# Causal mask of the stick-breaking attention by a mask matmul in place of a diagonal-seeded scan

## The chip, the cores and the metric

The kernel runs on one core of one Trainium2 chip. The metric is the device time of one execution in microseconds (us), median of several runs. Engines: PE is TensorE, ACT is ScalarE, DVE is VectorE, POOL is GpSimd, SP issues DMAs.

## The reference

Two transformer-like blocks run on one sequence of 512 tokens with model width 1024: a hybrid block (forgetting attention, causal convolution, gated feed-forward), then a state-space layer, and last a stick-breaking attention layer with 16 heads of 64. Only that last layer is touched. For a query t and a key s, with z the scaled logit, it computes

```python
z = einsum('bthd,bshd->bhts', q[:, lo:hi], k[:, :hi]) * scale
mask = (lo + arange(128))[:, None] > arange(hi)[None, :]      # strictly earlier keys
log_keep = where(mask, log_sigmoid(-z), 0.0)
after = cumsum(log_keep, axis=3, reverse=True) - log_keep     # sum over later allowed keys
a = exp(where(mask, log_sigmoid(z) + after, -inf))
out = einsum('bhts,bshd->bthd', a, v[:, :hi])
```

So each weight is sigmoid(z) of its key times the product of sigmoid(-z) over the allowed keys that come after it. Queries go in blocks of 128, so a block has 128, 256, 384 or 512 keys, and only its last 128 columns (the diagonal block) hold masked places.

## The kernel before, in words

Everything is in one launch and one core. Matrix products are done in three passes on operands split into a high and a low part (fp32r). A panel of weights is 1 MB; panels stream from HBM into `raw`, ACT makes the high part (line 189), DVE the low part (line 193), PE multiplies.

The last part of the program (line 1974 on) first makes keys, values and the first queries (loop of nine panels, lines 2290 to 2308 on DVE), and then runs the attention as a pipeline, written out by hand, over 32 units. A unit n is a pair of heads t = n // 4 and a query block qb = n % 4; both heads (e = 0, 1) are done in it. The stages of a unit are:

- `logits` on PE (line 2076): six matmuls, three for each head, that contract 64 rows each; the two heads lie in the two row halves of the array. They write PSUM banks 2 and 3. The width is nk = 128 (qb + 1) keys, but at least 256. The last matmul increments `z_done`.
- ACT waits for `z_done`, writes sigmoid(z) into `sig` (line 2258, shown as tile x) and sigmoid(-z) into `rest` (line 2262), and increments `keep`. PE waits for `keep` of unit n before the logits of unit n + 1.
- DVE scans `rest` from the last key to the first (line 2346), one scan for each head. The scan computes state = rest * state + own, starting from 0. `own` is a [128, 512] tile with zeros in its first 384 columns and the identity in its last 128, so the state is 0 at the masked places, becomes 1 at the diagonal and is multiplied on from there. It increments `rest`.
- POOL multiplies `sig` by the scanned `rest` shifted by one key (line 2049) and increments `am`. Column 512 of `rest` is the value to the right of the last key: 0.
- PE transposes the product (`turn`, line 2086), ACT copies it to SBUF (`take`, line 2233), PE multiplies with the values (`values`, line 2100), and increments `pv_done`.

Around these stages PE has filling work: the remaining query and gate projections (`project`, line 2123, until unit 27) and, after them, the first products of the output projection (`out_early` and `out_part`, line 2132). In iteration n PE does: logits of n, two k-tiles of the filler (six matmuls of 512 columns), turn of n - 2, two more k-tiles, values of n - 3. What ends the filler halves on ACT and DVE is lines 2239 and 2244 (ACT) and 2321 and 2316 (DVE); the gate is line 2332 and the split of its result lines 2250 and 2337.

The tile `exact` holds the first four of five constant matrices rounded to fp32r: identity, an upper triangle, and two masks with -1e30. It is made once at the start (line 585). The mask `neg_after` is -1e30 where column > row; `neg_from` is -1e30 where column >= row, and is not used. The first attention of the program (units from 127 to 214 us) adds `neg_after` to its own logits in PSUM by a matmul with the identity as weights; its lines are 798, 802 and 805:

```python
for e in range(2):
    mm = pe.matmul(ps[:, 2 + e, qb * P:nk], ident_r, exact[:, CST["neg_after"], :],
                   start=False, stop=True, skip_group_check=True)
```

`own` shares the 2 KB of a partition that `exact` has (line 132), and is written over it by DVE before the second attention (lines 2287 to 2289).

Of the kernel before, what the change touches and what calls it, by code (L numbers as in the profile page):

```python
# [15 lines left out]
F32 = mybir.dt.float32  # L16
F32R = mybir.dt.float32r
ALU = mybir.AluOpType
# [3 lines left out]
P = 128  # L22
S = 512
# [7 lines left out]
HD = 64  # L31
# [46 lines left out]
CST = dict(ident=0, upper=1, neg_after=2, neg_from=3, ones=4)  # L78
# [21 lines left out]
def build(nc, x_in, panels, ada, vecs, cst, w_f, w_dt, x_kept, ac_rows, out):  # L100
    ctx = ExitStack()
    with ctx:
        def sem(name):
            return ctx.enter_context(nc.semaphore(name))

        def sbuf(scope, name, shape, dt=F32):
            return scope.enter_context(nc.sbuf_tensor(name, shape, dt))

        def shared_sbuf(scope, first, then):

            with nc.sbuf_tensor(*first) as tensor:
                pass
            return [tensor] + [sbuf(scope, *one) for one in then]
# [15 lines left out]
        eps = sbuf(ctx, "eps", [P, 1])  # L129
        quad = sbuf(ctx, "quad", [P, 1])  # L130

        exact, own = shared_sbuf(ctx, ("exact", [P, 4, P], F32R), [("own", [P, S], F32)])
        ps = ctx.enter_context(nc.psum_tensor("ps", [P, 8, S], F32))
        MODB = 4
        ident = consts[:, CST["ident"], :]
        ones = consts[:, CST["ones"], :]
        ident_r = exact[:, CST["ident"], :]

        def v(name, i=None, n=None):
            a, w = VEC[name]  # L140
            if i is None:
                return vec[:, a:a + w]
            return vec[:, a + i:a + i + (n or 1)]
# [47 lines left out]
        def split_lo(e, c, i):  # L191
            e.wait_ge(hi_split, at(c + 1, i))
            e.tensor_tensor(wlo[:, c % 2, :, :], raw[:, c % 2, :, :], whi[:, c % 2, :, :].bitcast(F32),  # L193
                            ALU.subtract).then_inc(lo_split, 1)
# [478 lines left out]
        with ExitStack() as kept:  # L673
            with ExitStack() as seg:
# [5 lines left out]
                u = sbuf(seg, "u", [P, CT, CK - 1 + S])  # L680
# [654 lines left out]
        with ExitStack() as seg:  # L1335
# [24 lines left out]
            k = 0  # L1360
# [613 lines left out]
        with ExitStack() as seg:  # L1974
# [4 lines left out]
            QS = 3  # L1979
# [8 lines left out]
            sig = x[:, 0:6, :].rearrange("p (a h) s -> p a h s", a=3)  # L1988
            og = x[:, 6:8, :]
            amt = ada_raw[:, 0, :, :].rearrange("p k n -> p (k n)").rearrange("p (a h s) -> p a h s", a=2, h=2)  # L1990
            z2 = ada_raw[:, 1, :, :].rearrange("p k n -> p (k n)").rearrange("p (a s) -> p a s", a=4)
            rest = sbuf(seg, "rest", [P, 2, 2, S + 1])
            h0 = rest[:, 0, :, 0:S]
            pre3 = pre_norm(v("kv_norm"), "kvsc", "kvsh", hhi, hlo, h0, ps[:, 7, :])
            pre4 = pre_norm(v("norm2", KT, KT), "ssc", "ssh", h2hi, h2lo, h0, ps[:, 7, :], slot=2)
            fin = counting(bank_done=KT - 1, x_new1=KT, sq_ready=KT, ss_used=KT, std_ready=1, rs_ready=1, spread=1,
                           out_ready=KT, out_stored=16 * KT)
            fsq = v2[:].rearrange("p a (b s) -> p (a b) s", b=2)
            B = {k: sem("b_" + k) for k in ("own", "z_done", "sig", "keep", "rest", "am", "t_done", "amt",
                                            "pv_done", "og", "ohi", "olo", "half", "khi", "qhi", "qfree", "zsig",  # L2000
                                            "zfree")}
            sb0 = FIRST["sb_out"]
# [2 lines left out]
            def place(j):  # L2005

                if j in (7, 8):
                    return c0 + 15 - j
                if j < 9 or j >= 16:
                    return c0 + j  # L2010
                return FIRST["z2"] + (j - 9) // 2 if j % 2 else FIRST["q2"] + (j - 8) // 2
# [6 lines left out]
            with nc.Block() as block:  # L2018
                @block.sync
                def _(sp):  # L2020
# [8 lines left out]
                    for j in range(6, 20):  # L2029
                        sp.wait_ge(lo_split, c0 + j - 1)  # L2030
                        sp.dma_start(raw[:, (c0 + j) % 2, :, :].rearrange("p t n -> p (t n)"),
                                     panels[place(j)]).then_inc(w_landed[(c0 + j) % 2], 16)
                    sp.wait_ge(B["t_done"], NU)
                    sp.wait_ge(B["olo"], KT)
                    sp.dma_start(x[:], x_kept).then_inc(x_back, 16)
# [6 lines left out]
                def _(pool):  # L2042
# [3 lines left out]
                    for n in range(NU):  # L2046
                        nk = (n % TB + 1) * P
                        pool.wait_ge(B["rest"], n + 1)
                        pool.tensor_tensor(sig[:, n % 3, :, 0:nk], sig[:, n % 3, :, 0:nk],  # L2049
                                           rest[:, n % 2, :, S - nk + 1:S + 1], ALU.mult).then_inc(B["am"], 1)  # L2050

                @block.tensor
                def _(pe):
# [9 lines left out]
                    def logits(n):  # L2063
                        t, qb = divmod(n, TB)
                        nk = (qb + 1) * P
                        nw = max(nk, 2 * P)
                        if n == 0:
                            pe.wait_ge(pair_free[1], (q0 + 7) // 2 + 2)
                        else:
                            pe.wait_ge(B["keep"], n)  # L2070
                        if qb == 0 and t >= 2:
                            pe.wait_ge(B["qfree"], t - 1)
                        for u, (q, k) in enumerate(((qhi, khi), (qhi, klo), (qlo, khi))):
                            for e in range(2):
                                r0 = HD * e
                                mm = pe.matmul(ps[:, 2 + e, 0:nw], q[r0:r0 + HD, t % QS, qb * P:nk],  # L2076
                                               k[r0:r0 + HD, t, 0:nw], start=u == 0, stop=u == 2, skip_group_check=True)
                        mm.then_inc(B["z_done"], 1)

                    def turn(n):  # L2080
# [93 lines left out]
                    for b in (5, 6, 7, 4):  # L2174
# [4 lines left out]
                        for k2i in range(2):  # L2179
                            mm = out_part(0, b, k2i)  # L2180
                    mm.then_inc(panels_used, 1)
                    for b in (5, 6, 7, 4):
                        for k2i in range(2):
                            mm = out_part(1, b, k2i)
# [3 lines left out]
                    for k2i in range(2):  # L2188
                        for b in range(8):
                            mm = out_part(2, b, k2i)  # L2190
# [3 lines left out]
                    for j, b in enumerate(ORDER):  # L2194
                        for k2i in range(2):
                            mm = out_part(3, b, k2i)
# [85 lines left out]
                def _(dve):  # L2282
# [1 line left out]
                    pre4["coefs"](dve)  # L2284
                    pre3["dve"](dve)
                    split_lo(dve, c0 + 1, 0)
                    dve.memset(own[:, 0:S - P], 0.0).then_inc(B["own"], 1)
                    dve.tensor_copy(own[:, S - P:S], ident).then_inc(B["own"], 1)
                    dve.memset(rest[:, :, :, S:S + 1], 0.0).then_inc(B["own"], 1)
                    for j in range(9):  # L2290
                        pair = (q0 + j) % 2
                        bank = ps[:, 2 * pair:2 * pair + 2, :]
# [13 lines left out]
                            pre4["dve"](dve, 4 * j, 4 * j + 4)  # L2306
                        if j == 7:
                            read_mod(dve, NADA - 2, NADA)
                    dve.wait_ge(B["own"], 3)

                    def turn_half(mh):
                        name, i, b, c = half_of(mh)
# [27 lines left out]
                    for n in range(NU + 6):  # L2340
                        if n < NU:
                            nk = (n % TB + 1) * P
                            dve.wait_ge(B["keep"], n + 1)
                            for e in range(2):
                                turned = rest[:, n % 2, e, S - nk:S][:, ::-1]
                                scan = dve.tensor_tensor_scan(turned, turned, own[:, S - nk:S][:, ::-1], 0.0,  # L2346
                                                              ALU.mult, ALU.add)
                            scan.then_inc(B["rest"], 1)
                        if n == 0:
                            split_lo(dve, c0 + 10, 0)  # L2350
                        if n >= STEPS and n % STEPS == 0 and n // STEPS <= HALVES:
                            turn_half(n // STEPS - 1)
                        if n >= 7 and (n - 3) % 4 == 0:
                            gate((n - 3) // 4 - 1)
                        if n >= 9 and (n - 5) % 4 == 0:
                            out_lo((n - 5) // 4 - 1)
# [119 lines left out]
```

## Time and profile before

| | |
|---|---|
| median of 3 runs | 1405.9 us (1403.95, 1405.9, 1407.66) |
| the profiled execution: its own time / its span | 1407.66 us / 1405.9 us |
| PE busy | 1340.1 us, 95% of the span |
| DVE, ACT, POOL busy | 821.7, 588.5, 409.5 us |
| the attention pipeline, 1198 to 1357 us | PE busy 157.36 of 159 us |

The profile is of one execution. Its span is what the instructions cover; its own time is the device time of the same execution, 1.8 us more. It is the slowest of the three runs. That its span has the same figure as the median is a coincidence. Busy times are summed over instructions that overlap in the pipeline of PE, so two matmuls in a row may each show 390 ns and start 230 ns apart; the start times tell what one costs.

### The profile page before, as it was taken

Reading aid. Unit: us, or ns where it says so; the run is one execution under the profiler, and the core shown is the slowest. Engines: PE = TensorE matmul, PEld = TensorE weight load, DVE = VectorE, ACT = ScalarE, POOL = GpSimd, SP = SyncE. Lnnn points to the kernel's source line nnn. Section 1 sums busy time; section 2 is a strip of 40 time slices with the busy share of each in tenths; the row PEclk is TensorE's granted clock in tenths of the full one; section 3 lists DMA queues with packets and bytes.
Section 4 is the critical chain, followed back from the end, with each engine's and each line's share of the span. In section 5 each row is a group of like instructions: output and inputs, shape, how many; then the busy total and the mean of one; then the engine's idle time right before and its main releaser. Section 6 shows DMA issues by size and latency. Waiting matters only on the chain. (4 is left out here: it accounts for less than half of the span.)

```text
span 1405.9 us, 19406 instructions
## 1 busy us (share of the span) xinstructions
PE 1340.1 (95%) x7840; PEld 1066.5 (76%) x7840; DVE 821.7 (58%) x966; ACT 588.5 (42%) x849; POOL 409.5 (29%) x191
## 2 busy tenths in 40 slices
PE   5999999889999999999999999999899999999996
PEld 3778867668888888887788876777787799777775
DVE  2789974576555554324657665787832842566643
ACT  4323656342222222122444447777632422555551
POOL 0000000149978879999100000000000050233310
PEclk9999999889999999999799999999999999999998
DMA  9434062115444455554132233334222342111121
GB/s 383 147 146 150 31 242 89 61 64 205 179 179 179 179 209 194 198 203 152 56 128 90 92 116 102 121 106 132 88 89 90 124 170 91 66 54 38 61 90 60
DMA packets 41350, 181.12 MB, mean 129 GB/s; under 512 B 3392, under 2 KB 20160, under 8 KB 21312
## 3 DMA queue, kind: packets, MB, share of 16 engines
q1 hardware_dynamic: 40128, 171.73, 34.0%
q10 hardware_dynamic: 1152, 8.39, 1.7%
q8 instruction: 51, 0.84, 0.2%
q14 instruction: 19, 0.16, 0.0%
HBM read 173.75 MB, written 6.36 MB: 128 GB/s over the span
## 5 line engine op out<-in xcount | busy, mean ns | idle before, releaser
L193 DVE TENSOR_TENSOR wlo<-raw,whi 128x2048 fp32r<-128x2048 f32 x95 | 253.1, 2665 | 171.0 <-ACT whi L189 168.5
L200 POOL TENSOR_TENSOR ada_raw<-ada_raw,cs 128x2048 f32<-128x2048 f32 x36 | 150.4, 4178 | 495.7 <-DVE h2lo L451 451.1
L271 PE MATMUL ps<-hhi,whi 128*128 128x512 f32 x640 | 252.0, 394 | 2.3 <-PEq L563 0.8
L271 PE MATMUL ps<-hhi,wlo 128*128 128x512 f32 x640 | 249.4, 390 | 0.0
L271 PE MATMUL ps<-hlo,whi 128*128 128x512 f32 x640 | 249.1, 389 | 0.0
L189 ACT ACTIVATE whi<-raw 128x2048 fp32r<-128x2048 f32 x95 | 181.6, 1912 | 144.4 <-PE ps L1312 91.3
L209 POOL TENSOR_TENSOR ada_raw<-ada_raw 128x1024 f32<-128x1024 f32 x72 | 164.4, 2283 | 5.6
L271 PEld LDWEIGHTS ps<-hhi,whi 128*128 128x128 f32 x640 | 120.2, 188 | 28.6 <-issue 2.4
L271 PEld LDWEIGHTS ps<-hhi,wlo 128*128 128x128 f32 x640 | 120.1, 188 | 25.6
L271 PEld LDWEIGHTS ps<-hlo,whi 128*128 128x128 f32 x640 | 120.2, 188 | 24.4
L2049 POOL TENSOR_TENSOR x<-x,rest 128x256 f32<-128x256 f32 (+3 forms) x32 | 49.0, 1532 | 153.3 <-DVE rest L2346 153.3
L2346 DVE TENSOR_TENSOR_SCAN rest<-rest,own 128x128 f32<-128x128 f32 (+3 forms) x64 | 60.9, 992 | 50.7 <-ACT rest L2262 50.3
L1262 ACT ACTIVATE fg<-ps 128x512 f32<-128x512 f32 x22 | 13.2, 599 | 174.3 <-PE ps L271 174.3
L739 DVE SCALAR_TENSOR_TENSOR cv<-u,vec,cv 128x512 f32<-128x512 f32 x120 | 81.9, 746 | 0.4
L1277 DVE TENSOR_TENSOR fg<-ps,fg 128x512 f32<-128x512 f32 x22 | 15.2, 692 | 100.5 <-ACT fg L1262 100.5
L1811 DVE SCALAR_TENSOR_TENSOR xbc<-ps,vec,xbc 128x511 f32 (+5 forms) x72 | 48.4, 743 | 41.9 <-ACT xbc L1666 41.8
L433 POOL TENSOR_TENSOR x<-x,y 128x512 f32<-128x512 f32 x4 | 5.1, 1273 | 226.2 <-DVE y L419 226.2
L1312 PE MATMUL ps<-flo,whi 128*128 (+1 forms) x176 | 70.2, 399 | 0.0
L1312 PE MATMUL ps<-fhi,whi 128*128 (+1 forms) x176 | 69.7, 396 | 0.0
L1312 PE MATMUL ps<-fhi,wlo 128*128 (+1 forms) x176 | 69.0, 392 | 0.0
L1503 PE MATMUL ps<-hhi,whi 128*128 128x512 f32 x128 | 55.4, 432 | 0.4 <-DVE wlo L193 0.4
L1503 PE MATMUL ps<-hlo,whi 128*128 128x512 f32 x128 | 50.4, 394 | 0.0
(373 smaller groups left out, 2756.4 us busy)
## 6 DMA issues: line engine op xcount, KB each, us to landing
raw<-panels SPq DMA_DIRECT2D x87, 1024.0 KB, 4.9
ada_raw<-ada SPq DMA_DIRECT2D x48, 1024.0 KB, 6.7
first<-ada SPq DMA_DIRECT2D x8, 1024.0 KB, 20.5
bc<-ac_rows SPq DMA_DIRECT2D x32, 256.0 KB, 3.7
raw<-panels ACTq DMA_DIRECT2D x8, 1024.0 KB, 5.1
x_kept<-x SPq DMA_DIRECT2D x2, 2048.0 KB, 9.6
x<-x_kept SPq DMA_DIRECT2D x2, 2048.0 KB, 8.0
x<-x_in SPq DMA_DIRECT2D x1, 2048.0 KB, 10.6
```

Source lines behind the costliest of these rows:

```text
L189: e.activation(whi[:, c % 2, :, :], raw[:, c % 2, :, :], ACT.Copy).then_inc(hi_split, 1)
L193: e.tensor_tensor(wlo[:, c % 2, :, :], raw[:, c % 2, :, :], whi[:, c % 2, :, :].bitcast(F32), ALU.subtract).then_inc(lo_split, 1)
L200: e.tensor_tensor(ada_raw[:, c % 2, :, :], ada_raw[:, c % 2, :, :], cs[:, which, :].unsqueeze(2).to_broadcast([P, KT, 256]), ALU.mult).the ...
L209: e.tensor_tensor((ada_acc[:, c % 2, :] if sums is None else sums).unsqueeze(1) if width == 1 else part, part, ada_raw[:, c % 2, width:2 * ...
L271: mm = e.matmul(ps[:, 2 * (qc % 2) + b, :], w[:, c % 2, 2 * k + b, :], src[part][:, k, :], **flags)
L739: dve.scalar_tensor_tensor(out=cv[:, j, :], in0=src, scalar=w, in1=cv[:, j, :], op0=ALU.mult, op1=ALU.add).then_inc(A["tap"], 1)
L1277: dve.tensor_tensor(fg[:, pair, :], ps[:, 2 * pair + 1, :], fg[:, pair, :], ALU.mult).then_inc(prod_ready, 1)
L1312: mm = pe.matmul(ps[:, b, :], w[:, c % 2, k2 * 8 + b, :], src[:, kt, :] if isinstance(i, int) else src[:, bass.ds(kt + i * 4, 1), :], star ...
L1503: mm = pe.matmul(ps[:, 2 * (qp % 2) + b, :], wt[:, cp % 2, 2 * kt + b, :], (hhi, hlo)[part][:, kt, :], start=(kt == 0 and j == 0), stop=(k ...
L1811: ins = dve.scalar_tensor_tensor(out=xbc[:, bass.ds(t, 1), s:S], in0=ps[:, 2 * pair + b, 0:S - s], scalar=vec[:, bass.ds(wc, 1)], in1=xbc[ ...
L2049: pool.tensor_tensor(sig[:, n % 3, :, 0:nk], sig[:, n % 3, :, 0:nk], rest[:, n % 2, :, S - nk + 1:S + 1], ALU.mult).then_inc(B["am"], 1)
L2346: scan = dve.tensor_tensor_scan(turned, turned, own[:, S - nk:S][:, ::-1], 0.0, ALU.mult, ALU.add)
```

## The change

The mask moves from the scan to PE. The six logit matmuls leave the accumulation open (stop=False), and one more matmul for each head, identity times `neg_from`, adds -1e30 to the masked places of the diagonal block; the second of them now increments `z_done`. With that, sigmoid(z) is 0 and sigmoid(-z) is 1 at masked places. The scan starts from 1 and adds zero from a [128, 1] tile read with stride 0 in place of `own`; column 512 of `rest` is set to 1. The tile `own` and its two writes go, `exact` keeps its memory to the end.

```diff
-        exact, own = shared_sbuf(ctx, ("exact", [P, 4, P], F32R), [("own", [P, S], F32)])
+        exact = sbuf(ctx, "exact", [P, 4, P], F32R)
...
+            zero = sbuf(seg, "zero", [P, 1])
...
-                                mm = pe.matmul(ps[:, 2 + e, 0:nw], q[r0:r0 + HD, t % QS, qb * P:nk],
-                                               k[r0:r0 + HD, t, 0:nw], start=u == 0, stop=u == 2, skip_group_check=True)
+                                pe.matmul(ps[:, 2 + e, 0:nw], q[r0:r0 + HD, t % QS, qb * P:nk],
+                                          k[r0:r0 + HD, t, 0:nw], start=u == 0, stop=False, skip_group_check=True)
+                        for e in range(2):
+                            mm = pe.matmul(ps[:, 2 + e, qb * P:nk], ident_r, exact[:, CST["neg_from"], :],
+                                           start=False, stop=True, skip_group_check=True)
                         mm.then_inc(B["z_done"], 1)
...
-                    dve.memset(own[:, 0:S - P], 0.0).then_inc(B["own"], 1)
-                    dve.tensor_copy(own[:, S - P:S], ident).then_inc(B["own"], 1)
-                    dve.memset(rest[:, :, :, S:S + 1], 0.0).then_inc(B["own"], 1)
+                    dve.memset(zero[:], 0.0).then_inc(B["zero"], 1)
+                    dve.memset(rest[:, :, :, S:S + 1], 1.0).then_inc(B["zero"], 1)
...
-                    dve.wait_ge(B["own"], 3)
+                    dve.wait_ge(B["zero"], 2)
...
-                                scan = dve.tensor_tensor_scan(turned, turned, own[:, S - nk:S][:, ::-1], 0.0,
-                                                              ALU.mult, ALU.add)
+                                scan = dve.tensor_tensor_scan(turned, turned, zero[:, 0:1].to_broadcast([P, nk]),
+                                                              1.0, ALU.mult, ALU.add)
```

## Rows read from the trace of the kernel before

**Rows 1.** The page: slices of the span, and the chain that ended last

```profile
PEclk9999999889999999999799999999999999999998
PE 21%; DVE 1%; ACT 0%; issue 0%; DVEq 0%; ACTq 0%
PE ps L2123 6%; PE ps L268 3%; PE ps L2132 3%; PE ps L271 3%; PE ps L2100 2%; PE ps L2076 1%; PE ps L2086 1%; PE ps L478 1%; DVE y L2372 0%; PE ps L336 0%; PE ps L316 0%; ACT v L2212 0%; DVE rsq L330 0%; PE ps L217 0%; DVE x L2365 0%
```

**Rows 2.** Windows, pipeline and tail: us, busy (instructions) by engine, PEclk, DMA, GB/s

```profile
1198.00:1357.00 159.00, 157.36 (x1055) 116.80 (x1052) 96.46 (x100) 88.92 (x126) 49.03 (x32) 1.00 0.16 54
1357.00:1406.00 49.00, 37.79 (x216) 29.90 (x216) 18.29 (x21) 11.37 (x14) 0.00 (x0) 0.88 0.23 86
```

**Rows 3.** Waits of PE from 1195 to 1358 us: total, times, longest

```profile
PE ps L2132 <- DVE ada_raw L2316: 1.0, 1, 1.0
PE ps L2123 <- ACT v L2212: 0.7, 1, 0.7
```

**Rows 4.** Timeline, one unit of the second attention: start us, duration us, instruction

```profile
1214.36 0.28 PE L2076 MATMUL ps<-khi,qlo 64*128 64x256 f32 x2
1214.57 0.49 PE L2123 MATMUL ps<-h2hi,whi 128*128 128x512 f32 x1
1214.68 0.38 ACT L2258 ACTIVATE x<-ps 128x256 f32<-128x256 f32 x1 [1.72 <-PE ps L2076]
1214.90 0.40 PE L2123 MATMUL ps<-h2lo,whi 128*128 128x512 f32 x1
1215.13 0.39 PE L2123 MATMUL ps<-h2hi,wlo 128*128 128x512 f32 x1
```

**Rows 5.** Timeline, one unit of the first attention, with its mask pair L805

```profile
127.14 0.28 PE L798 MATMUL ps<-k1hi,q1lo 64*128 64x256 f32 x2
127.25 0.28 PE L802 MATMUL ps<-ncx,sel 64*128 64x256 f32 x2
127.46 0.30 PEld L805 LDWEIGHTS ps<-exact 128*128 128x128 f32 x2
127.46 0.44 PE L805 MATMUL ps<-exact 128*128 128x128 f32 x2
127.74 0.44 PE L851 MATMUL ps<-hhi,whi 128*128 128x512 f32 x1
128.02 0.39 PE L851 MATMUL ps<-hlo,whi 128*128 128x512 f32 x1
128.25 0.40 PE L851 MATMUL ps<-hhi,wlo 128*128 128x512 f32 x1
```

**Rows 6.** Line 805 by source: duration ns min/median/max, first and last start

```profile
L805 PEld LDWEIGHTS ps<-exact x32: 186/188/190, 127.5 to 213.9; 128*128 128x128 f32 x32
L805 PE MATMUL ps<-exact x32: 272/302/329, 127.5 to 214.0; 128*128 128x128 f32 x32
```

**Rows 7.** Timeline around the logits of unit 0

```profile
1197.69 1.02 ACT L2212 ACTIVATE v<-ps 128x1024 f32<-128x1024 f32 x1 [7.16 <-PE ps L268]
...
1197.93 0.28 PE L2076 MATMUL ps<-khi,qlo 64*128 64x256 f32 x2
1198.61 0.38 ACT L2258 ACTIVATE x<-ps 128x256 f32<-128x256 f32 x1
...
1198.86 0.47 PE L2123 MATMUL ps<-h2hi,whi 128*128 128x512 f32 x1 [0.66 <-ACT v L2212]
```

**Rows 8.** Timeline around the logits of unit 29

```profile
1335.77 0.28 PE L2076 MATMUL ps<-khi,qlo 64*128 64x256 f32 x2
1337.03 0.50 PE L2132 MATMUL ps<-hhi,whi 128*128 128x512 f32 x1 [0.98 <-DVE ada_raw L2316]
```

**Rows 9.** DVE's three writes before the attention, and its next wait

```profile
1106.42 0.38 DVE L2287 MEMSET own<- 128x384 f32 x1
1106.72 0.16 DVE L2288 COPY own<-consts 128x128 f32<-128x128 f32 x1
1107.96 1.23 DVE L2295 TENSOR_TENSOR klo<-ps,khi 128x1024 fp32r<-128x1024 f32 x1 [1.06 <-ACT khi L2216]
```

**Rows 10.** DVE groups by shape, 1196 to 1352 us: busy, mean ns, idle before

```profile
L2346 DVE TENSOR_TENSOR_SCAN rest<-rest,own 128x512 f32<-128x512 f32 x16 | 18.7, 1213 | 23.1 <-ACT rest L2262 23.1
L2346 DVE TENSOR_TENSOR_SCAN rest<-rest,own 128x128 f32<-128x128 f32 x16 | 17.1, 1108 | 9.6 <-ACT rest L2262 9.2
L2346 DVE TENSOR_TENSOR_SCAN rest<-rest,own 128x384 f32<-128x384 f32 x16 | 14.9, 972 | 17.8 <-ACT rest L2262 17.8
L2346 DVE TENSOR_TENSOR_SCAN rest<-rest,own 128x256 f32<-128x256 f32 x16 | 10.2, 676 | 0.2 <-ACT rest L2262 0.2
```

More of the change, by code:

```diff
@@ L1998, in build @@
             fsq = v2[:].rearrange("p a (b s) -> p (a b) s", b=2)
-            B = {k: sem("b_" + k) for k in ("own", "z_done", "sig", "keep", "rest", "am", "t_done", "amt",
+            B = {k: sem("b_" + k) for k in ("zero", "z_done", "sig", "keep", "rest", "am", "t_done", "amt",
                                             "pv_done", "og", "ohi", "olo", "half", "khi", "qhi", "qfree", "zsig",
```

## The prediction

> **What bounds the kernel now.** I read the page first, then windows over the part that the change touches, then the waits, then single units in the timeline. The page's chain that ended last, merged by line, is nearly all PE, and the attention's lines (2123, 2076, 2086, 2100, 2132) stand at its head; of ACT and DVE it has next to nothing [rows 1]. The window over the 32 units says the same from the other side: PE is busy 157.36 of 159 us at a granted clock of 1.00, while DVE has 96.46, ACT 88.92 and POOL 49.03 [rows 2]. The waits show that PE stood still for another engine twice in this stretch, for 0.7 and 1.0 us [rows 3]. So in the attention PE is the bound. An instruction added to PE there moves the end by the time that it takes in PE's queue; time taken from DVE moves nothing unless it ends one of those two waits.
>
> **The change part by part.**
>
> *The mask pair on PE.* Each of the 32 units gets two matmuls of 128 columns with full 128 x 128 weights, so 64 matmuls and 64 weight loads. The same pair exists in the trace, in the first attention: line 805, 32 matmuls and 32 weight loads, the medians 302 ns and 188 ns [rows 6]. Those are durations of overlapping instructions, so the sum would be too high with them; I read what the pair costs from start times. Without a mask pair, from the last logit pair's start to the start of the third filler matmul of 512 columns: 1214.36 to 1215.13, 0.77 us [rows 4]. With one, from the last 64-row pair (line 802) over line 805 to the third matmul of 512 columns: 127.25 to 128.25, 1.00 us [rows 5]. The shapes at both ends are alike, so a pair costs 1.00 - 0.77 = 0.23 us. The inside agrees: the step from 64-row to full-array matmuls is 0.21 us in both (1214.36 to 1214.57, 127.25 to 127.46), that is, the change adds no switch of that kind, it only comes before the mask instead of before the filler; the pair then takes 0.28 (127.46 to 127.74); and the first filler matmul, which stood 0.33 before the next (1214.57 to 1214.90), stands 0.28 (127.74 to 128.02) since the stall after the switch is now the mask's. 0.28 - 0.05 = 0.23.
>
> Two bounds. Above: nothing is absorbed, 0.28 for each pair. Below: a matmul costs only its columns. From 512 columns in 0.23 us (1214.90 to 1215.13) a column is 0.45 ns, 128 columns 0.058, a pair 0.115 us. The weight loads speak against the lower one: the two of line 805 end 0.30 us after the first starts, with 0.19 for one, so the second starts 0.11 us after the first [rows 5], and twice 0.11 is 0.22. A weight load every 0.11 us, not 128 columns, sets the pace. I take 0.23.
>
> The page "TensorE: Matmul & The Clock Gate" of the Trainium skill, in its section "Back-to-back issue gap", puts a sustained stream of weight load plus matmul at N=128 at about 81 ns for one; by that the pair is 0.16 us and an estimate for 30 pairs is 4.9 us. The trace's own pair is dearer.
>
> *Which pairs lie on the path.* Not all. After the logits of unit 0 (last pair at 1197.93) PE waits 0.66 us for ACT's copy of the values, which ends at 1198.71, and the first sigmoid starts at 1198.61, behind the same copy in ACT's queue [rows 7]: a mask pair that ends by about 1198.4 is hidden. After the logits of unit 29 (1335.77) PE waits 0.98 us for DVE's line 2316, whose inputs are older than these logits [rows 8]: hidden too. That leaves 30 pairs: 30 x 0.23 = 6.9 us. All other filler matmuls begin without a wait.
>
> *The longer way to the sigmoids.* `z_done` comes 0.28 us later against the logits, while all of PE's later work comes 0.23 later, so every chain through ACT, DVE and POOL back to PE loses 0.05 us of slack. ACT has 1.72 us of idle time before the sigmoid [rows 4], DVE 50.7 us of idle time before its scans in all [rows 10], and PE's list of waits has no wait for line 2262, 2346, 2049 or 2233 at all [rows 3]. What waits on ACT behind line 2258 (line 2262, the copy of the transposed weights, the sigmoid of the gate) is moved with PE. Cost: nothing. If one of these were tight, it would be 0.05 x 32 = 1.6 us at most.
>
> *The scan.* The same 64 scans, same lengths, in place, reversed; only the second operand changes from a tile to one element with stride 0, and the start value to 1. No row shows a scan with such an operand. The shortest group is 676 ns for 256 columns, 1213 for 512; the group for 128 columns has 1108 because it often meets POOL's long product [rows 10]. I take no difference. From below, a faster scan gains nothing, since PE doesn't wait for it. From above see the rivals.
>
> *DVE's setup.* Two writes go (0.38 and 0.16 us), a tiny one comes; right after them DVE waits 1.06 us for ACT's keys [rows 9]. They lay in that wait: nothing.
>
> *Sum.* 6.9 us. On the profiled execution: span 1405.9 to 1412.8, own time 1407.66 to 1414.6. That execution was the slowest of the three and 1.8 us over the median, so against the median 1405.9 I expect 1412.8, +0.49%. The tail after 1357 us is moved as it is, at its clock of 0.88 [rows 2].
>
> **The rivals.**
>
> *A pair costs only its columns, or hides in the stall after the switch of row halves; not slower.* This is the lower bound: 30 x 0.115 = 3.5 us, 1409.4. If in addition the whole 0.10 us by which the first filler step exceeds a steady one (0.33 against 0.23, rows 4) were taken up, almost nothing would be left, about 1406. It decides below 4.2 us, that is, under 0.14 us for a pair. For it: the matmul itself has a quarter of the filler's columns, and the weights are the same for both heads. Against it: line 805 has the same weights twice as well, and loads them twice, 32 for 32 [rows 6]. Chance 0.13.
>
> *PE gets back what it waited for, and the end comes no later.* The two waits sum to 1.66 us [rows 3]; if a shorter DVE (setup and scan) ended both, the time would be 1405.9 + 7.4 - 1.7 = 1411.6 with all 32 pairs counted; to come out faster by 0.3% the pipeline would have to lose 4.2 us that the rows don't have. Nothing speaks for it. Faster over 0.3%: 0.03, for things outside this argument (another tail, a clock that falls less than in the slices of 9, 8 and 7 in rows 1).
>
> *The scan becomes slow and DVE the bound; slower by far.* A tile of four units has two scans of each length, 2 x (1213 + 972 + 676 + 1108) = 7.9 us of DVE; 32 units 60.9. If the operand with stride 0 doubled it, DVE would have 96.46 + 60.9 = 157 us in 159 and would set the pace together with the splits: some 10 us over the mask's, 1423. Chance 0.03.
>
> *Nothing is absorbed.* 32 x 0.28 = 9.0 us, 1414.9. Chance 0.12; the forecast itself (5.5 to 8 us) 0.69.
>
> **How the numbers follow.** A measurement of this kernel tells about 0.3% (4.2 us) from no change; the three runs span 3.7 us. Slower by over 0.3% is the forecast, the unabsorbed pair and the slow scan, less what the spread of the medians (some 1.5 us either way) takes off the forecast: 0.81. Within 0.3%: the column rival and that part, 0.16. Faster: 0.03. The range goes from the column rival less a little, 1409.0, to the unabsorbed pair plus the spread, 1416.0.
>
> **What would show it.** In the changed profile: 64 matmuls and 64 weight loads on the mask's line, the pair taking about 0.28 us up to the next filler matmul, and 1.00 us from the last logit pair to the third filler matmul; the last of the pair releasing line 2258's successor in place of the logits; the wait after unit 0 down from 0.66 to about 0.4 us and the one after unit 29 from 0.98 to about 0.7; the scans' mean by shape as before with DVE's idle time before them no smaller; the stretch from unit 0 to the last values longer by 6.9 us, everything ahead of it and behind it unchanged. The prediction is wrong if new waits of PE for the transposed weights or for `keep` appear, if the scans have other durations, if a pair takes under 0.14 us net, or if the parts ahead of 1190 us move by more than a microsecond.

## The result and the profile after

The changed kernel takes 1414.08 us (median of 4 runs, 1412.84 to 1416.69) against 1405.38 us for the kernel before in its 4 runs: ratio 1.0069, interval 1.0044 to 1.0095. The prediction was 1412.8 us, +0.49%, range 1409.0 to 1416.0. A later comparison of the same two kernels in more rounds (run e10 below) gave 1.0053, 1.0033 to 1.0073. The profiled execution of the changed kernel took 1413.45 us, with a span of 1411.7; it isn't among the four, nor is one more of 1419.2 us.

The lines of the changed kernel are shifted: the logits are line 2077, the mask pair 2080, the two sigmoids 2262 and 2266, the filler 2127 and 2136, the transposes 2090, the scan 2349.

The mask pair by its source line (duration in ns, minimum, median, maximum), in the changed kernel:

```profile
L2080 PEld LDWEIGHTS ps<-exact x64: 186/188/189, 1197.1 to 1350.4; 128*128 128x128 f32 x64
L2080 PE MATMUL ps<-exact x64: 272/302/328, 1197.1 to 1350.5; 128*128 128x128 f32 x64
...
  ACT x L2262: 54.2, 24
```

These are the durations of line 805 in [rows 6], for twice as many instructions. The first sigmoid now waits for this line.

One unit of 256 columns in the changed kernel's timeline, the place of [rows 4]:

```profile
1213.99 0.28 PE L2077 MATMUL ps<-khi,qlo 64*128 64x256 f32 x2
1214.20 0.44 PE L2080 MATMUL ps<-exact 128*128 128x128 f32 x2
1214.47 0.44 PE L2127 MATMUL ps<-h2hi,whi 128*128 128x512 f32 x1
...
1214.67 0.39 ACT L2262 ACTIVATE x<-ps 128x256 f32<-128x256 f32 x1 [2.09 <-PE ps L2080]
1214.75 0.40 PE L2127 MATMUL ps<-h2lo,whi 128*128 128x512 f32 x1
...
1214.99 0.39 PE L2127 MATMUL ps<-h2hi,wlo 128*128 128x512 f32 x1
```

From the last logit pair to the third filler matmul: 1213.99 to 1214.99, 1.00 us, where the same place took 0.77 us in [rows 4]. The steps are 0.21, 0.27, 0.28 and 0.24: a switch to the full array, the pair, a first filler matmul with a short stall, a steady one. In the 30 units without a wait, the pair's step is 0.27 or 0.28 and the first filler's 0.28 to 0.30 (before: 0.33 to 0.35).

One distance grew by more than the 0.28 us that the prediction gave it. The first sigmoid starts 0.68 us after the last logit pair (1213.99 to 1214.67), where it was 0.32 (1214.36 to 1214.68 [rows 4]): 0.36 later, since the 0.21 us of the switch now lie ahead of `z_done` too. Wherever ACT is ready for it in both kernels, the growth is 0.36 or 0.37 us, whatever the number of keys.

Whether all of it reached the end is read from a stretch with clear marks: from unit 0's last logit pair to the first transpose of unit 31. Before it begins at 1197.93 [rows 7] and ends at 1352.87, here at 1196.90 and 1358.63. The last marks, first of the kernel before, then of the changed one:

```profile
1352.87 1.03 PE L2086 MATMUL ps<-consts,x 128*128 128x128 f32 x8
```

```profile
1358.63 1.04 PE L2090 MATMUL ps<-consts,x 128*128 128x128 f32 x8
```

The stretch went from 154.94 to 161.73 us, +6.79. What follows is as long as it was: 1405.9 - 1352.87 = 53.0 us, and 1411.7 - 1358.63 = 53.1 us. The work ahead was 1.0 us shorter in this execution (1197.93 against 1196.90); so the spans differ by only 5.8 us. Of that 1.0 us, 0.9 were there by the last mask pair of the first attention (213.84 against 212.93), long before the two writes of DVE that the change takes out at 1106 us.

The waits of PE in this part of the changed kernel (total, times, longest), against [rows 3], and the windows over the pipeline and the tail, against [rows 2]:

```profile
PE ps L2136 <- DVE ada_raw L2319: 0.6, 1, 0.6
PE ps L2127 <- ACT v L2216: 0.3, 1, 0.3
```

```profile
1197.00:1363.00 166.00, 165.10 (x1119) 124.22 (x1116) 94.93 (x101) 88.56 (x126) 49.02 (x32) 1.00 0.15 52
1363.00:1411.70 48.70, 37.58 (x216) 29.71 (x214) 18.07 (x21) 11.37 (x14) 0.00 (x0) 0.88 0.23 87
```

No wait is new. The two old ones are shorter by 0.4 us each. That those two pairs were hidden is seen from the start times, after unit 0 and after unit 29:

```profile
1196.90 0.28 PE L2077 MATMUL ps<-khi,qlo 64*128 64x256 f32 x2
...
1197.84 0.47 PE L2127 MATMUL ps<-h2hi,whi 128*128 128x512 f32 x1 [0.29 <-ACT v L2216]
```

```profile
1341.10 0.28 PE L2077 MATMUL ps<-khi,qlo 64*128 64x256 f32 x2
...
1342.35 0.50 PE L2136 MATMUL ps<-hhi,whi 128*128 128x512 f32 x1 [0.61 <-DVE ada_raw L2319]
```

From the logits to the filler are 0.94 and 1.25 us with the pair between them, and 0.93 and 1.26 before [rows 7], [rows 8]. The granted clock is 1.00 and 0.88 as before.

DVE's scans by shape (busy, mean ns, idle before), against [rows 10]:

```profile
L2349 DVE TENSOR_TENSOR_SCAN rest<-rest,zero 128x512 f32<-128x512 f32 x16 | 18.7, 1212 | 25.2 <-ACT rest L2266 25.2
...
L2349 DVE TENSOR_TENSOR_SCAN rest<-rest,zero 128x128 f32<-128x128 f32 x16 | 15.6, 1011 | 11.2 <-ACT rest L2266 11.2
L2349 DVE TENSOR_TENSOR_SCAN rest<-rest,zero 128x384 f32<-128x384 f32 x16 | 14.6, 951 | 21.9 <-ACT rest L2266 21.9
L2349 DVE TENSOR_TENSOR_SCAN rest<-rest,zero 128x256 f32<-128x256 f32 x16 | 10.2, 676 | 0.5 <-ACT rest L2266 0.5
```

The operand with stride 0 costs what the tile cost (1212 against 1213, 676 against 676 ns). DVE's idle time before the scans grew from 50.7 to 58.8 us.

### The profile page after: what moved, and what is told of

It is laid out like the page before. It is cut to its first block and busy times, and to the rows that moved or that the text cites. A ratio compares the mean times of both kernels' runs of the same rounds, so it can differ in the third digit from the quotient of the medians.

```text
span 1411.7 us, 19533 instructions
## 1 busy us (share of the span) xinstructions
PE 1347.8 (95%) x7904; PEld 1073.8 (76%) x7904; DVE 820.0 (58%) x965; ACT 588.4 (42%) x849; POOL 407.1 (29%) x191
## 5 line engine op out<-in xcount | busy, mean ns | idle before, releaser
L193 DVE TENSOR_TENSOR wlo<-raw,whi 128x2048 fp32r<-128x2048 f32 x95 | 257.9, 2714 | 174.6 <-ACT whi L189 172.0
L200 POOL TENSOR_TENSOR ada_raw<-ada_raw,cs 128x2048 f32<-128x2048 f32 x36 | 144.8, 4024 | 499.5 <-DVE h2lo L451 451.0
L209 POOL TENSOR_TENSOR ada_raw<-ada_raw 128x1024 f32<-128x1024 f32 x72 | 168.1, 2334 | 5.6
L2349 DVE TENSOR_TENSOR_SCAN rest<-rest,zero 128x128 f32<-128x128 f32 (+3 forms) x64 | 59.0, 963 | 58.9 <-ACT rest L2266 58.9
```

Source lines behind the costliest of these rows:

```text
L200: e.tensor_tensor(ada_raw[:, c % 2, :, :], ada_raw[:, c % 2, :, :], cs[:, which, :].unsqueeze(2).to_broadcast([P, KT, 256]), ALU.mult).the ...
L209: e.tensor_tensor((ada_acc[:, c % 2, :] if sums is None else sums).unsqueeze(1) if width == 1 else part, part, ada_raw[:, c % 2, width:2 * ...
L2349: scan = dve.tensor_tensor_scan(turned, turned, zero[:, 0:1].to_broadcast([P, nk]), 1.0, ALU.mult, ALU.add)
```

## The experiments

The theory: the loss is the mask pairs on PE and nothing else, 0.23 us for each of 30 exposed ones, and their price is that of their fp32r weight loads. The rivals: the other half of the change (scan and setup) carries a part; the columns set the price; the place of the pair, or the switch between 64-row and full matmuls, sets it; something outside the attention is slower. All runs, with the stretch between the same two marks in each profile (it was the better measure, since the work ahead of it varies from run to run). Most ratios rest on 4 to 12 runs of the kernel, those of e11 and e12 on two:

| kernel | stretch, us | ratio to before | interval |
|---|---|---|---|
| before | 154.9 | 1 | |
| changed | 161.7 | 1.0069 | 1.0044 to 1.0095 |
| e10, changed again | 161.7 | 1.0053 | 1.0033 to 1.0073 |
| e1, mask pair alone | 161.8 | 1.0038 | 1.0024 to 1.0053 |
| e2, scan alone | 154.9 | 0.9992 | 0.9976 to 1.0007 |
| e3, mask 256 columns wide | 161.8 | 1.0048 | 1.0032 to 1.0065 |
| e4, four pairs | 182.1 | 1.0200 | 1.0178 to 1.0221 |
| e5, pair between the logits | 171.4 | 1.0124 | 1.0107 to 1.0141 |
| e6, pair in bf16 | 157.2 | 1.0009 | 0.9997 to 1.0020 |
| e9, four pairs in bf16 | 167.2 | 1.0085 | 1.0068 to 1.0102 |
| e11, 12 more, 64 weight columns | 183.5 | 1.0213 | 1.0183 to 1.0243 |
| e12, 12 more, 64 moving columns | 203.2 | 1.0348 | 1.0318 to 1.0378 |
| e7, before, first attention's pair in bf16 | 154.9 | 0.9972 | 0.9961 to 0.9982 |
| e8, changed, both attentions' pairs in bf16 | 157.4 | 0.9992 | 0.9982 to 1.0003 |

**e1: the mask pair alone.** Against the kernel before; `own` moves to a buffer that is free by then.

```diff
+            own = ada_acc[:].rearrange("p a b -> p (a b)")
...
+                        for e in range(2):
+                            mm = pe.matmul(ps[:, 2 + e, qb * P:nk], ident_r, exact[:, CST["neg_from"], :],
+                                           start=False, stop=True, skip_group_check=True)
```

> The PE half of the change alone: the mask pair stays, the scan keeps its seed tile own (moved to another buffer). I read the stretch from unit 0's last logit pair to the transposes of unit 31 (154.94 us before, 161.73 after). Theory (30 exposed pairs of 0.23 us): 161.7 us, that is all of the +6.8, and a time of 1.005 times before. Rival (part of the loss comes from the changed scan): less than 160.5 us.

161.8 us: the whole of the +6.8. Its ratio, 1.0038, is lower than that of the changed kernel at the same stretch; the intervals overlap.

**e2: the scan alone.** Against the changed kernel, the mask pair is taken out again; the kernel then leaves out the masking, and only its time is of use.

```diff
-                        for e in range(2):
-                            mm = pe.matmul(ps[:, 2 + e, qb * P:nk], ident_r, exact[:, CST["neg_from"], :],
-                                           start=False, stop=True, skip_group_check=True)
```

> The DVE half alone: the scan starts from 1 and adds the stride-0 zero, no mask pair on PE, so the masked places are not masked and the output is another one. Theory: PE never waits for the scan, stretch 154.9 us as before, ratio 1.000; the scans by shape 1212, 951, 676 and about 1010 ns. Rival (the scan carries part of the loss, as the medians' +8.7 against the stretch's +6.8 could hint): stretch above 156 us, ratio 1.0015 or more.

154.9 us and ratio 0.9992: the DVE half neither costs nor brings anything. Its scans by shape:

```profile
L2346 DVE TENSOR_TENSOR_SCAN rest<-rest,zero 128x512 f32<-128x512 f32 x16 | 18.7, 1213 | 23.0 <-ACT rest L2263 23.0
...
L2346 DVE TENSOR_TENSOR_SCAN rest<-rest,zero 128x128 f32<-128x128 f32 x16 | 17.1, 1106 | 9.6 <-ACT rest L2263 9.2
```

The group of 128 columns has 1106 ns, as before, and not the 1010 that I had expected from the changed kernel: that mean is shorter there because the scans meet POOL's products at another moment, which moves with PE. The timelines show it: two scans of 128 columns in a row take 0.74 us with POOL idle (unit 0), 2.32 to 2.35 us where 1.73 to 1.75 of them lie beside a product of POOL (before and e2), and 2.10 to 2.12 where 1.50 to 1.53 do (changed).

**e4 and e3: more pairs, and wider ones.**

```diff
-                        for e in range(2):
-                            mm = pe.matmul(ps[:, 2 + e, qb * P:nk], ident_r, exact[:, CST["neg_from"], :],
-                                           start=False, stop=True, skip_group_check=True)
+                        for again in range(4):
+                            for e in range(2):
+                                mm = pe.matmul(ps[:, 2 + e, qb * P:nk], ident_r, exact[:, CST["neg_from"], :],
+                                               start=False, stop=again == 3, skip_group_check=True)
```

> Four mask pairs for each unit in place of one (the mask is added four times). Theory (each 128-column matmul waits for its own weight load, one every 0.11 us): three more pairs of 0.22 us in 32 units, 21.1 us, less the 0.9 us that is left of the two waits: stretch 181.9 us, 1.019 times before. Rival (only columns count, 0.058 us for 128, and the rest of the pair's 0.23 is paid once for each unit): 3 x 0.115 x 32 - 0.9 = 10.1 us more, stretch 171.9 us, 1.012 times before.

For e3 the part `neg_after` of `exact` is set to zero before the second attention, and the matmul takes it and `neg_from` as one operand:

```diff
+                        lo = max(qb - 1, 0) * P
...
-                            mm = pe.matmul(ps[:, 2 + e, qb * P:nk], ident_r, exact[:, CST["neg_from"], :],
+                            mm = pe.matmul(ps[:, 2 + e, lo:nk], ident_r,
+                                           exact[:, CST["neg_from"] - (1 if qb else 0):CST["neg_from"] + 1, :],
```

> The mask matmul is 256 columns wide in the 24 units with 256 keys or more (128 zeros, then the mask), same weights, same number of loads. Theory (weight loads set the pace): 256 columns take 0.117 us against 0.11 for a load, so 24 x 2 x 0.007 = 0.3 us more: stretch 162.1 us, 1.005 times before. Rival (columns set it): 24 x 0.115 = 2.8 us more, stretch 164.5 us, 1.0068 times before.

Both came out for the theory: 182.1 us (181.9 against the rival's 171.9), and 161.8 us (162.1 against 164.5). In e4's timeline the eight matmuls of a unit:

```profile
1217.98 0.28 PE L2077 MATMUL ps<-khi,qlo 64*128 64x256 f32 x2
1218.18 0.97 PEld L2081 LDWEIGHTS ps<-exact 128*128 128x128 f32 x8
1218.19 1.11 PE L2081 MATMUL ps<-exact 128*128 128x128 f32 x8
...
1219.13 0.45 PE L2128 MATMUL ps<-h2hi,whi 128*128 128x512 f32 x1
```

From 1218.19 to 1219.13 there are eight steps: 0.1175 us each on the mean. The first pair takes 0.27 to 0.28 of it, as in the changed kernel, so a further matmul takes (0.94 - 0.27) / 6 = 0.11 us; the 20.4 us that e4's stretch has over the changed kernel's, with the 0.9 us left of the two waits, make 0.11 for each of 192 too.

In e3 the steps of a unit are others, and their sum is the same:

```profile
1224.10 0.50 PE L2082 MATMUL ps<-exact 128*128 128x256 f32 x2
1224.44 0.39 PE L2130 MATMUL ps<-h2hi,whi 128*128 128x512 f32 x1
1224.67 0.39 PE L2130 MATMUL ps<-h2lo,whi 128*128 128x512 f32 x1
```

The wide pair takes 0.34 us until the filler, and the first filler matmul 0.23, without a stall: 0.57 us. With 128 columns they are 0.28 and 0.29, 0.57 as well. At 256 columns the columns alone would take as long as the loads (an estimate of 0.23 us for a pair, from 0.23 for 512 columns), so e3 shows that the second 128 columns are free, not that the pair's own step is unchanged.

**e5: the pair between the first and the second logit pair.**

```diff
                         for u, (q, k) in enumerate(((qhi, khi), (qhi, klo), (qlo, khi))):
...
+                            if u == 0:
+                                for e in range(2):
+                                    pe.matmul(ps[:, 2 + e, qb * P:nk], ident_r, exact[:, CST["neg_from"], :],
+                                              start=False, stop=False, skip_group_check=True)
```

> The mask pair stands between the first and the second logit pair, not after the third, so PE goes from 64-row matmuls to full ones and back once more in each unit. Theory (the pair at the end adds no switch and its first step is the stall that the filler had): the step into the pair is 0.21 us, the pair 0.28, against 0.115 for the step it replaces, so 0.37 us a unit or more if the way back also stalls: 30 x 0.37 = 11 us, stretch 166 us or more, 1.008 times before. Rival (the place doesn't matter, a pair costs 0.23 anywhere): stretch 161.7 us, 1.005.

171.4 us, +16.5 over before; the rival is out, and the theory's 0.37 us for a unit was its lower bound. The unit in e5's timeline, up to the first filler's weight load:

```profile
1216.59 0.39 PE L2077 MATMUL ps<-khi,qhi 64*128 64x256 f32 x2
...
1216.90 0.44 PE L2081 MATMUL ps<-exact 128*128 128x128 f32 x2
...
1217.27 0.38 PE L2077 MATMUL ps<-klo,qhi 64*128 64x256 f32 x2
...
1217.49 0.28 PE L2077 MATMUL ps<-khi,qlo 64*128 64x256 f32 x2
1217.70 0.19 PEld L2128 LDWEIGHTS ps<-h2hi,whi 128*128 128x128 f32 x1
```

From the first logit pair to the filler are 1.11 us. In the kernel before, the same unit begins here and has its filler at 1214.57 [rows 4], 0.55 us later:

```profile
1214.02 0.39 PE L2076 MATMUL ps<-khi,qhi 64*128 64x256 f32 x2
```

So the pair costs 0.56 us here, 0.33 more than at the end of the logits: the way back to 64-row matmuls stalls as well. The "TensorEngine Tiling (Array Packing)" page of the Trainium skill, section "Key Properties", says that changing the tiling mode drains the engine. The trace agrees so far as each change of rows comes with a stall, with the 0.33 us for one more change there and back beside it; that the stall is a drain, the trace doesn't show.

**e6 and e9: the pair in bf16, once and four times.** The tile `mask16` holds identity and mask in bf16.

```diff
+            mask16 = sbuf(seg, "mask16", [P, 2, P], mybir.dt.bfloat16)
...
-                            mm = pe.matmul(ps[:, 2 + e, qb * P:nk], ident_r, exact[:, CST["neg_from"], :],
+                            mm = pe.matmul(ps[:, 2 + e, qb * P:nk], mask16[:, 0, :], mask16[:, 1, :],
...
+                    dve.tensor_copy(mask16[:, 0, :], ident).then_inc(B["zero"], 1)
+                    dve.tensor_copy(mask16[:, 1, :], consts[:, CST["neg_from"], :]).then_inc(B["zero"], 1)
```

> The mask pair has bf16 operands (identity and mask, both exact enough in bf16), accumulated on the fp32r logits. Theory (the weight load of an fp32r matmul sets the pace): with a shorter load the pair costs between its columns, 0.115 us, and 0.23, I say 0.15: stretch 159.4 us, 1.0035 times before. Rival (the fixed cost after the switch of row halves sets it, whatever the type): stretch 161.7 us, 1.005.

> Four bf16 mask pairs for each unit. What does a further bf16 pair cost? Theory (its pace is its columns, 0.053 us for 128, since the load no longer sets it): 3 x 0.107 x 32 = 10.3 us over the one bf16 pair, less the 1.2 us that is left of the two waits: stretch 166.3 us, 1.0081 times before. Rival (bf16 hides its pair only once, in the stall after the switch of row halves, and a further pair costs as much as in fp32r): 3 x 0.22 x 32 - 1.2 = 19.9 us, stretch 177.1 us, 1.016.

e6: 157.2 us, +2.3 over before, 0.08 us for each of 30 pairs, about half of my 0.15. The unit in e6's timeline:

```profile
1215.24 0.28 PE L2079 MATMUL ps<-khi,qlo 64*128 64x256 f32 x2
...
1215.45 0.28 PE L2082 MATMUL ps<-mask 128*128 128x128 bf16 x2
...
1215.55 0.48 PE L2129 MATMUL ps<-h2hi,whi 128*128 128x512 f32 x1
...
1215.87 0.39 PE L2129 MATMUL ps<-h2lo,whi 128*128 128x512 f32 x1
```

The pair takes 0.10 us until the filler starts; the filler's stall (0.32) stays. With e9 the pace is plain, eight matmuls from 1206.58 to 1207.01:

```profile
1206.58 0.62 PE L2083 MATMUL ps<-mask 128*128 128x128 bf16 x8
1206.98 0.19 PEld L2130 LDWEIGHTS ps<-h2hi,whi 128*128 128x128 f32 x1
1207.01 0.48 PE L2130 MATMUL ps<-h2hi,whi 128*128 128x512 f32 x1
```

0.054 us each, about half of the 0.11 of a further fp32r matmul. e9's stretch, 167.2 us, is near the 166.3 of the theory and far from 177.1. The section "Weight-path perf modes — Fast Weight Load (FWL) and DoubleRow" of the Trainium skill's "TensorE: Matmul & The Clock Gate" says that weights of types other than fp32 load faster when there are 128 of them; the trace agrees as far as bf16 goes (a load shows 97 ns in e6 against 188).

**e11 and e12: is it the load?** bf16 changes the load and the matmul at once, so these two take them apart in fp32r. After the pair come twelve more matmuls, in e11 with half the weights, in e12 with half the moving columns.

```diff
+                        for again in range(6):
+                            for e in range(2):
+                                mm = pe.matmul(ps[0:HD, 2 + e, qb * P:nk], ident_r[:, 0:HD], exact[:, CST["neg_from"], :],
+                                               start=False, stop=again == 5, skip_group_check=True)
```

```diff
+                                mm = pe.matmul(ps[:, 2 + e, nk - HD:nk], ident_r, exact[:, CST["neg_from"], HD:P],
+                                               start=False, stop=again == 5, skip_group_check=True)
```

> After the mask pair, twelve more fp32r matmuls a unit with the same 128 columns but only 64 columns of weights (the mask is added again for queries 0 to 63). Why does an fp32r mask matmul take 0.1175 us and a bf16 one 0.054? Theory (the fp32r weight load, whose time goes with its columns of weights): about 0.06 us for each, 0.72 a unit and a little for the switch to 64 columns: stretch 183 to 188 us. Rival (an fp32r matmul of under 256 columns is slow by itself, whatever its weights): 0.1175 each, 1.41 a unit: stretch 206 us or more.

> After the mask pair, twelve more fp32r matmuls a unit with all 128 columns of weights and only 64 moving columns (the last 64 of the diagonal block). Theory (the weight load sets the pace): 0.1175 us each as for 128 columns, 1.41 a unit, less 0.9 in all: stretch 206 us. Rival (fp32r columns pass at half pace when there are under 256 of them): 0.06 each, 0.72 a unit: stretch 184 us.

The twelve and the next matmul, in e11's timeline and then in e12's:

```profile
1211.12 0.80 PEld L2084 LDWEIGHTS ps<-exact 128*64 128x64 f32 x12
1211.18 0.88 PE L2084 MATMUL ps<-exact 128*64 128x128 f32 x12
...
1211.90 0.45 PE L2131 MATMUL ps<-h2hi,whi 128*128 128x512 f32 x1
```

```profile
1211.75 1.42 PEld L2084 LDWEIGHTS ps<-exact 128*128 128x128 f32 x12
1211.81 1.48 PE L2084 MATMUL ps<-exact 128*128 128x64 f32 x12
...
1213.11 0.47 PE L2131 MATMUL ps<-h2hi,whi 128*128 128x512 f32 x1
```

Half the weights: 0.72 us for twelve, 0.060 each, with 128 moving columns. Half the moving columns: 1.30 us, 0.108 each. Stretches 183.5 us (183 to 188 expected) and 203.2 us (206 expected, 184 by the rival). So the weight load sets the pace of the fp32r mask matmul. That e12 fell 2.8 us short of its 206 is the 0.1175 that I took from e4: it held the first pair's longer step. With 0.11 for each of 384 matmuls, less the 0.9 us of the waits, it would have been 203.1. e11's 0.060 is also what 128 columns take by themselves (0.058, from 0.23 for 512), so a load of 64 columns may be shorter still.

**e7 and e8: the bf16 pair where it was already paid for.** The first attention has 16 such pairs (line 805), in both kernels. The edit is shown for e7, against the kernel before; e8 gives `exact` the same type in the changed kernel.

```diff
-        exact, own = shared_sbuf(ctx, ("exact", [P, 4, P], F32R), [("own", [P, S], F32)])
+        exact, own = shared_sbuf(ctx, ("exact", [P, 4, P], mybir.dt.bfloat16), [("own", [P, S], F32)])
```

> The kernel before, with the constants of the first attention's mask pair (line 805) in bf16 in place of fp32r. Theory (an fp32r weight load sets the pair's pace, a bf16 one doesn't): a pair is 0.15 us shorter, as in the second attention (0.23 against 0.08); 12 of the 16 pairs lie in the stretch from 127 to 190 us where PE is busy 62.87 of 63 us: 1.8 us less between the first and the last pair, up to 2.4 with all 16, ratio 0.9985. Rival (DVE, 57.10 of those 63 us busy, or the loads of the last units take the gain): no change, ratio 1.000.

> The changed kernel with both attentions' mask pairs in bf16. Theory: the second attention's stretch 157.2 us as with bf16 there alone, the first attention 1.8 to 2.4 us shorter: +2.3 - 2.0 = +0.3 us, ratio 1.000. Rival (nothing is gained in the first attention): +2.3 us, ratio 1.0016.

e7 is faster than both kernels: 1403.78 us against 1407.92 for the kernel before on the same chip, 0.9972. The pairs of line 805 in e7, against [rows 6], and the wait of PE that shrank beside them:

```profile
L805 PEld LDWEIGHTS ps<-exact x32: 95/97/99, 127.6 to 211.0; 128*128 128x128 bf16 x32
L805 PE MATMUL ps<-exact x32: 219/224/230, 127.6 to 211.1; 128*128 128x128 bf16 x32
```

```profile
PE ps L229 <- DMA ada_raw<-ada: 1.5, 2, 0.7
```

From the first pair to the last, 127.46 to 213.84 before, are 86.4 us; in e7, 127.56 to 211.03, 83.5. That is 2.9 us less, more than the 2.4 I had given as the most. Fifteen pairs of 0.15 make 2.25; a wait for two adaLN panels, 2.3 us before, is 1.5 and makes up the rest. That wait isn't the edit's: it is 1.9 us in the changed kernel, 1.7 in e10 and 2.5 in e9, with line 805 as it was, and 2.1 in e8, with the edit. The time between the two pairs less this wait is 84.0 to 84.2 us in before, changed, e10 and e9, and 82.0 and 82.1 in e7 and e8. So the pairs gained 2.1 us. Another 0.9 us of the medians' 4.1 lies behind the attention: from the last mark to the end e7 takes 52.1 us at a granted clock of 0.93, the kernel before 53.0 at 0.89. e3 and e6 have the same 52.1 us, at 0.93 and 0.92, without this edit, so nothing speaks for the edit as its cause. So 2.1 us, 0.15%, are shown for bf16, and e8's ratio against e6's (0.9992, 1.0009) is in keeping with that; e7's interval ends a little beyond it, and what makes the rest in its other runs isn't shown. e8, with both attentions in bf16, has the second stretch at 157.4 us and the ratio 0.9992, about e6's and e7's effects together (1.0009 x 0.9972 = 0.9981; the intervals overlap).

**e10: the changed kernel again.**

> The changed kernel once more, unchanged, in more rounds, because its first four runs gave 1.0069 times before (1.0044 to 1.0095) where its stretch in the profile accounts for 6.8 us, 1.0048. Theory (the mask pairs are all of it): ratio 1.0048, interval inside 1.003 to 1.0065, stretch 161.7 us. Rival (the change costs something more, outside the attention): ratio 1.0065 or more.

1.0053, stretch 161.7 us. The interval, 1.0033 to 1.0073, holds 1.0048 and also reaches past the rival's 1.0065, so this run alone doesn't exclude 2 us outside the attention; e1 and e3, with the same work on PE, at 1.0038 and 1.0048, speak against it.

## Why the prediction was right

*What bounds.* PE, as read from the windows and the waits. e4 shows it best: 192 more matmuls in 32 units moved the end by what they take in PE's queue, with the instructions of DVE, ACT and POOL unchanged. e2 shows the counterpart: nothing on DVE's side moved it.

*The price of a pair.* Predicted 0.23 us from the first attention's pair; the changed kernel has 1.00 against 0.77 us in a unit, the same. It was the start times that gave it. The medians of 302 and 188 ns, taken as costs, would have given 0.6 us for a pair and 18 us in all.

*The two bounds.* The argument against the lower bound, that weight loads every 0.11 us set the pace, held in four runs (e3, e4, e11, e12). The upper bound, nothing absorbed, did not occur: the first filler's step is 0.28 to 0.30 instead of 0.33 to 0.35 in all 30 units.

*Which pairs lie on the path.* Thirty of 32: the waits after units 0 and 29 shrank from 0.7 and 1.0 to 0.3 and 0.6 us, near the 0.4 and 0.7 that were given, and the filler behind each starts no later against the logits than before. 6.79 us were measured over the stretch for a sum of 6.9.

*Slack, scan and setup at nothing.* No new wait of PE; scans of equal duration where POOL is idle; e2 at 0.9992. But the size behind the slack was wrong: the sigmoids come 0.36 us later against the logits, not 0.28, so a chain over ACT and DVE loses 0.13 us a unit and not 0.05. With one of these chains tight it would have been up to 0.13 x 32 = 4.2 us, not 1.6. It cost nothing because PE waited for none of them.

*The median.* 1412.8 forecast, 1414.08 measured. The stretch accounts for 6.8 us of the 8.7 between the medians; the rest is inside the spread of four runs each (3.7 and 3.9 us), and the second comparison gave 1.0053. That the forecast came within 1.3 us of this median is partly luck: the median of the kernel before is itself 1405.38 here and 1407.3 in e10's comparison.

*A sign of being wrong that came up.* The prediction named a shift of over a microsecond ahead of 1190 us as such a sign. The logits of unit 0 moved by 1.03 us. The bound was too tight: the same mark lies at 1195.8 us in e2 and at 1202.1 in e9, which don't touch the work before 1106 us either.

*Two small sums.* The two waits of 0.66 and 0.98 us make 1.64, not 1.66. Eight tiles of 7.9 us of scans make 63.5 us of durations; the 60.9 beside it is the busy time, in which overlapping scans count once. Neither moves a bound or a chance.

Nothing in the sum failed. What was off was in the expectations behind it: a bf16 pair costs 0.08 us and not 0.15, and a pair between the logits 0.56 and not 0.37. The first because I put it between the floor of the columns, 0.115, and 0.23, where bf16 sits on the floor (0.054 for each matmul in e9) and some 0.03 us less is paid in e6 (0.09 or 0.10 us until the filler, whose step is 0.31 or 0.32); the second because no row of before showed a way back from full to 64-row matmuls inside a unit.

## What to carry to other kernels

Where one engine is busy for 99% of a stretch, work moved to it from an idle one is paid in full, even 64 small instructions; look for the same instruction elsewhere in the trace and take its price from start to start, with the steps before and after it. A constant matmul added to an accumulation (mask, bias) can have bf16 operands if nothing hangs on its rounding, whatever type the rest of the accumulation has; here that took two thirds off its price. And put it where the tile shape changes anyway, or beside matmuls of its own shape.

## What the runs showed of the hardware

- In a row of fp32r matmuls with 128 columns of weights, one takes 0.11 us at 64 (e12) and at 128 moving columns (e4), and a pair with 256 costs in all what a pair with 128 does (e3). With 64 columns of weights it takes 0.060 us at 128 moving columns (e11). The same 128 x 128 matmul in bf16 takes 0.054 us (e9).
- A pair of full matmuls between 64-row matmuls costs 0.33 us more than behind them, 0.56 against 0.23 (e5). Going from 128 to 64 columns of weights and back shows no such stall (e11: 0.28 us for the pair ahead and 0.28 for the filler behind, as in the changed kernel).
- With the change from 64-row to full matmuls ahead of its release, an engine waits longer than the pair costs PE: the sigmoids came 0.36 us later for a pair of 0.23.
- Two matmuls in a row with the same weights load them twice, in fp32r (64 loads for 64 matmuls in the changed kernel) and in bf16 (32 for 32 on line 805 in e7).
- A scan on DVE takes the same time with a [128, 1] operand of stride 0 as with a tile (1212 and 1213 ns for 512 columns). Beside a product of POOL it takes longer: 2.34 us in place of 0.74 for two scans of 128 columns.
